# One moving operand of 512 columns for the high and low part of h in the first products of FFN and MLP

## What is computed

```python
def swiglu(h, w_gu, w_down):
    gate, up = jnp.split(h @ w_gu, 2, axis=-1)      # w_gu: 1024 x 5632
    return (jax.nn.silu(gate) * up) @ w_down        # w_down: 2816 x 1024
...
x = x + 0.5 * swiglu(rms_norm(x, norm_ffn1[i]), w_ffn1_gu[i], w_ffn1_down[i])
...
# MLP of the second network: relu(h @ w_up) ** 2 @ w_down, w_up: 1024 x 4096
```

## Time and profile before

| | |
|---|---|
| median of 3 runs | 1770.35 us (1768.21 to 1771.86) |
| profiled execution, its own time | 1772.11 us |
| its span, first to last instruction | 1770.4 us |
| mean granted TensorE clock | 0.981 |
| instructions | 31231, of them 13254 matmuls |
| raw weights | 264 units, 4.9 us median from issue to landing |

### The profile page before, as it was taken

One profiled execution on the slowest core, in us unless ns is written; L12 is line 12 of the kernel. 1 busy time (PEld: TensorE's weight loads), 2 busy tenths in 40 slices (PEclk: granted clock), 3 DMA queues, 4 the chain that ended last, 5 costly groups with the idle time before them and its releaser, 6 DMA issues.

```text
span 1770.4 us, 31231 instructions
## 1 busy us (share of the span) xinstructions
PE 1700.2 (96%) x13254; PEld 1639.6 (93%) x13254; DVE 1077.2 (61%) x1057; ACT 803.8 (45%) x942; POOL 161.1 (9%) x123
## 2 busy tenths in 40 slices
PE   7999998999999999999999999888999999989997
PEld 7999985899999999989999998768999989989997
DVE  7565676375648755486554777564655566466553
ACT  5343557353435534365343544444444455444342
POOL 1000122100002000011000243220000001100000
PEclk9999999999999999999999999789999999999999
DMA  7545451155443544445545345003454435225550
GB/s 297 193 166 189 167 190 48 72 215 195 181 174 143 217 187 185 171 178 197 214 152 204 143 177 190 1 24 120 143 191 176 179 128 187 91 101 201 177 187 24
DMA packets 39637, 282.36 MB, mean 159 GB/s; under 512 B 4416, under 2 KB 4544, under 8 KB 5760
## 3 DMA queue, kind: packets, MB, share of 16 engines
q1 hardware_dynamic: 39168, 279.59, 42.6%
q0 software_dynamic: 384, 1.51, 0.2%
HBM read 280.04 MB, written 1.05 MB: 159 GB/s over the span
## 4 chain that ended last, share of the span: by engine, by line
PE 88%; DVE 6%; ACT 3%; DMA 1%; POOL 1%; issue 1%; SPq 0%; DVEq 0%; ACTq 0%; POOLq 0%
PE ps L312 27%; PE ps L313 27%; PE ps L314 27%; DVE w_lo L1342 1%; PE ps L396 1%; ACT arena L1154 1%; ACT w_hi L970 1%; PE ps L610 1%; PE ps L654 1%; DMA raw<-weights 1%; DVE hT_lo L1354 0%; POOL arena L2011 0%; DVE arena L1643 0%; DMA arena<-nsa_tables 0%; DVE X L1481 0%
## 5 line engine op out<-in xcount | busy, mean ns | idle before, releaser
L312 PE MATMUL ps<-hT_hi,w_hi 128*128 128x256 f32 x2504 | 715.7, 286 | 22.6 <-DVE hT_lo L1354 18.0
L313 PE MATMUL ps<-hT_lo,w_hi 128*128 128x256 f32 x2504 | 710.8, 284 | 0.0
L314 PE MATMUL ps<-hT_hi,w_lo 128*128 128x256 f32 x2504 | 710.5, 284 | 0.0
L1342 DVE TENSOR_TENSOR w_lo<-raw,w_hi 128x2048 fp32r<-128x2048 f32 x264 | 601.0, 2300 | 138.6 <-ACT w_hi L970 138.5
L970 ACT ACTIVATE w_hi<-raw 128x2048 fp32r<-128x2048 f32 x264 | 495.0, 1902 | 52.0 <-DMA raw<-weights 46.0
L312 PEld LDWEIGHTS ps<-hT_hi,w_hi 128*128 128x128 f32 x2504 | 482.4, 193 | 26.1 <-DVE w_lo L1342 11.2
L313 PEld LDWEIGHTS ps<-hT_lo,w_hi 128*128 128x128 f32 x2504 | 482.9, 193 | 0.8 <-issue 0.7
L314 PEld LDWEIGHTS ps<-hT_hi,w_lo 128*128 128x128 f32 x2504 | 482.9, 193 | 0.0
L312 PE MATMUL ps<-hid_hi,w_hi 128*128 128x256 f32 x1272 | 360.5, 283 | 3.6 <-DVE hid_lo L1442 2.6
L313 PE MATMUL ps<-hid_lo,w_hi 128*128 128x256 f32 x1272 | 361.0, 284 | 0.0
L314 PE MATMUL ps<-hid_hi,w_lo 128*128 128x256 f32 x1272 | 356.1, 280 | 0.0
(11 more groups left out here) (257 smaller groups left out, 1451.5 us busy)
## 6 DMA issues: line engine op xcount, KB each, us to landing
raw<-weights SPq DMA_DIRECT2D x264, 1024.0 KB, 4.9
X<-x SPq DMA_DIRECT2D x2, 512.0 KB, 6.8
out<-X SPq DMA_DIRECT2D x4, 256.0 KB, 2.1
arena<-p POOLq DMA_DIRECT2D x2, 256.0 KB, 5.9
arena<-counts POOLq DMA_DIRECT2D x1, 512.0 KB, 5.5
arena<-nsa_tables POOLq DMA_DIRECT2D x1, 448.0 KB, 7.1
const<-constants SPq DMA_DIRECT2D x1, 427.0 KB, 9.6
cols<-parameters SPq DMA_DIRECT2D x1, 213.5 KB, 2.6
```

What stands on the lines that cost most here:

```text
L312: nc.tensor.matmul(dst, a_hi, b_hi, start=start, stop=False, skip_group_check=True)
L313: nc.tensor.matmul(dst, a_hi, b_lo, start=False, stop=False, skip_group_check=True)
L314: return nc.tensor.matmul(dst, a_lo, b_hi, start=False, stop=stop, skip_group_check=True)
L1342: nc.vector.tensor_tensor(unit_cols(w_lo, u, 0, UNIT), raw[:, r * UNIT:(r + 1) * UNIT], f(unit_cols(w_hi, u, 0, UNIT)), ALU.subtract).then ...
```

## The change

The high and low part of h now lie in one tensor, and `both(k)` gives chunk k of both as one moving operand of two runs of 256 columns. In `wide` one matmul multiplies it by w_hi into a whole bank: w_hi by h_hi goes to the first half, w_hi by h_lo to the second. A second matmul adds w_lo by h_hi to the first half. The halves are added afterwards: ScalarE copies the second halves of two banks to SBUF (`take_low`), VectorE adds the first ones (`add_low`) and signals `added` or `second_added`. A tile takes a whole bank now, so a block of the FFN takes four banks and the MLP's blocks alternate between banks 0, 1 and 2, 3.

The FFN's units are laid out anew: u holds the gate's columns, u+1 the up columns, each with all eight chunks. The first FFN block (`first_wide`) goes through both units chunk by chunk and waits for the second unit at the start; the second block lies in banks 4 to 7, which `down` enters afterwards. The last FFN block keeps the old form (`up` with two tiles into banks 0 and 1). The square in the MLP takes in the relu. The orders on ScalarE and VectorE at a stage's opening and in the loops are rewritten.

```diff
+        def both(k):
+            return hT[:].rearrange("p (a x) -> p a x", a=2)[:, :, k * TOKENS:(k + 1) * TOKENS]
+        LOW = [at(0, 512), at(512, 512)]
...
+            def wide(b, u, a, k):
+                nc.tensor.matmul(by_tile(bank(b)), unit_cols(w_hi, u, a, P), both(k), start=k == 0, stop=False, skip_group_check=True)
+                return nc.tensor.matmul(bank(b, 0, TOKENS), unit_cols(w_lo, u, a, P), chunk(hT_hi, k), start=False, stop=k == KC - 1, skip_group_check=True)
+            def up_wide(u, b0, t=None, mid={}):
+                unit_ready(u, t)
+                for k in range(KC):
+                    if k in mid:
+                        mid[k]()
+                    for m in range(2):
+                        mm = wide(b0 + m, u, (2 * k + m) * P, k)
+                mm.then_inc(unit_used.sem, 1)
+            def first_wide(us, banks, mid={}):
+                for k in range(KC):
+                    if k in mid:
+                        mid[k]()
+                    if k == 0:
+                        unit_ready(us[1])
+                    pe.wait_ge(*hT_ready.due(me))
+                    for j, u in enumerate(us):
+                        for m in range(2):
+                            mm = wide(banks[j] + m, u, (2 * k + m) * P, k)
+                        if k == KC - 1:
+                            mm.then_inc(unit_used.sem, 1)
...
-            def down(u, h, first, last, t=None, squares=False):
+            def down(u, h, first, last, t=None, squares=False, free=None):
...
+                    if free and b == 2:
+                        pe.wait_ge(*free)
...
             # TensorE, ffn
-                one(0, u0, mid={6: lambda: sums(s)})
-                one(1, u0 + 2, mid={2: lambda: spread(7)})
+                def one(u, t):
+                    pe.wait_ge(*added.due(me, turn=t))
+                    up_wide(u, 0, t)
+                    pe.wait_ge(*second_added.due(me, turn=t))
+                    up_wide(u + 1, 2, t)
+                    down(u + 2, 0, False, False, t)
+                first_wide([u0, u0 + 1], (0, 2), {6: lambda: sums(s)})
+                up_wide(u0 + 2, 4, None, {4: lambda: spread(7)})
+                pe.wait_ge(rstd_read.sem, norm_of[s] + 1 - plain)
+                up_wide(u0 + 3, 6)
+                pe.wait_ge(*added.due(me, 2))
+                down(u0 + 4, 0, True, False, free=second_added.due(me, 2))
...
             # TensorE, mlp
-                sums(s)
-                up([u0 + 2], 2, 2, None, False, mid={5: lambda: spread(7)})
-                down(u0 + 3, 0, True, False)
+                first_wide([u0, u0 + 1], (0, 4))
+                sums(s, 2)
+                up_wide(u0 + 2, 6, None, {2: lambda: spread(2)})
+                down(u0 + 3, 0, True, False, free=added.due(me, 3))
...
             # ScalarE, ffn: the opening, then a turn of the loop
+                take_low(0, 0, u0 + 2)
+                take_low(2, 1, u0 + 2)
+                split_to(u0 + 8)
+                take_low(4, 0, u0 + 3)
+                silu(0)
+                round_hidden(0)
+                split_to(u0 + 9)
+                silu(1)
+                take_low(6, 1, u0 + 4)
+                split_to(u0 + 10)
+                round_hidden(0, u0 + 5)
...
+                    take_low(0, 0, u + 1, t)
+                    split_to(u + 6, t)
+                    silu(j, t)
+                    split_to(u + 7, t)
+                    take_low(2, 1, u + 2, t)
+                    split_to(u + 8, t)
+                    round_hidden(0, u + 3, t)
...
             # VectorE, ffn: the opening, then a turn of the loop
+                split_to(u0 + 4)
                 mean_square(7)
+                add_low(gates[0], 0, 0, added)
+                add_low(second, 2, 1, second_added)
                 split_to(u0 + 5)
                 take_rstd(7)
+                scale(gates[0])
+                scale(second)
+                hidden(0)
+                add_low(gates[1], 4, 0, added)
+                scale(gates[1])
+                low_hidden(0)
+                split_to(u0 + 6)
+                add_low(second, 6, 1, second_added)
+                scale(second)
+                hidden(1)
+                split_to(u0 + 8)
+                low_hidden(0)
+                split_to(u0 + 10)
...
+                    add_low(gates[j % 2], 0, 0, added, t)
+                    scale(gates[j % 2], t)
+                    split_to(u + 6, t)
+                    add_low(second, 2, 1, second_added, t)
+                    scale(second, t)
+                    hidden(j, t)
+                    split_to(u + 7, t)
+                    low_hidden(0, t)
+                    split_to(u + 8, t)
...
             # VectorE, mlp: the opening
+                split_to(u0 + 5)
+                mean_square(2)
+                add_low(SUMS[0], 0, 0, added)
+                add_low(SUMS[1], 4, 1, added)
+                take_rstd(2)
+                squares(0)
+                low_hidden(0)
+                squares(1)
+                add_low(SUMS[0], 6, 0, added)
...
+            def take_low(b0, n, used, t=None):
+                act.wait_ge(unit_used.sem, used + (t.i * t.units if t else 0))
+                nc.scalar.activation(by_tile(LOW[n]), pair(b0, 1), ACT.Copy).then_inc(low_taken.sem, 1)
...
+            def add_low(dst, b0, n, sig, t=None):
+                dve.wait_ge(*low_taken.due(me, turn=t))
+                nc.vector.tensor_tensor(by_tile(dst), pair(b0, 0), by_tile(LOW[n]), ALU.add).then_inc(sig.sem, 1)
```

More of the change, by code:

```diff
@@ L443, in ffn @@
             def ffn(s, u0):
[L445 to L449, removed]
-                one(0, u0, mid={6: lambda: sums(s)})
-                one(1, u0 + 2, mid={2: lambda: spread(7)})
+                plain = sum(kind in ("stick", "pool") for kind, _ in stages[:s])
+                def one(u, t):
[4 more added lines that the diff above has]
+                    down(u + 2, 0, False, False, t)
@@ L461, in ffn @@
                 down(u + 3, HC, False, True)
             def mlp(s, u0):
[L466 to L474, removed]
@@ L487, in mlp @@
+                up_wide(u, 2)
+                added.due(me, 2)
                 down(u + 1, HC, False, False)
@@ L1011, in ffn, with silu @@
             def ffn(s, u0):
-                def one(j, u, t=None):
-                    more = t.i * t.units if t else 0
+                def silu(j, t=None):
+                    gate = sil[:, j % 2 * 512:j % 2 * 512 + 512]
                     act.wait_ge(*scaled.due(me, turn=t))
[L1017 to L1026, removed]
@@ L1033, in ffn, with one @@
                     for b in range(2):
-                        one(2 + b, u + 3 * b, t)
-                scaled.due(me, 2 * 3)
-                hid_ready.due(me, 2 * 3)
+                        one(b, u + 3 * b, t)
+                all_of(me, (scaled, hid_ready), 2 * 3)
                 split[me] += 3 * 6
                 u += 24
-                one(FFN_BLOCKS - 1, u)
+                split_to(u + 6)
+                silu(FFN_BLOCKS - 1)
+                split_to(u + 7)
+                round_hidden(HC)
             def mlp(s, u0):
[L1043 to L1051, removed]
-                    nc.scalar.activation(chunk(hid_hi, j % 2 * HC, HC), at(ACT_AT, 512), ACT.Copy).then_inc(hid_hi_done.sem, 1)
-                    split_to(ahead, t)
-                one(0, u0 + 1, u0 + 6)
-                one(1, u0 + 2, u0 + 7)
-                one(2, u0 + 3, u0 + 8, free=u0 + 4)
+                def one(b, u, t=None):
+                    take_low((b + 1) % 2 * 2, (b + 1) % 2, u + 1, t)
+                    split_to(u + 5, t)
+                    round_hidden((b + 1) % 2 * HC, u + 2, t)
+                    split_to(u + 6, t)
+                take_low(0, 0, u0 + 1)
+                take_low(4, 1, u0 + 2)
+                split_to(u0 + 7)
+                round_hidden(0)
+                take_low(6, 0, u0 + 3)
+                round_hidden(HC)
+                split_to(u0 + 8)
+                round_hidden(0, u0 + 4)
                 u = u0 + 4
```

132 lines of the change are left out of this document (78 added, 54 removed).

## The result

The changed kernel takes 1824.81 us (median of 4 runs, 1823.1 to 1828.33) against 1769.28 us of the kernel before on the same chip (1767.07 to 1771.86): 1.0316 times as long, interval 1.0294 to 1.0338. The forecast was 1820, slower. The profiled execution took 1828.33 us, 56.2 more than the profiled one before; the forecast of that difference was 49.4.

The account below looks back on a forecast made before the run. TensorE, working without holes, was taken as the bound. On the profiled 1772.11 us, -22.9 + 5.0 + 61.5 + 8.4 - 2.6 = +49.4 gave 1821.5, or 1819.7 as median; own range 1804 to 1836, wider range 1785 to 1840.

Parts of the forecast that it names:

- Pace of a group: FFN and MLP matmul groups: 347.2 ns instead of 360, 12.8 ns less in 1792 groups, 22.9 us won.
- Rival (c): Matmul groups: the two-run operand streams at the pace of two matmuls, nothing won, 1843 us; chance 0.11.
- rival (d): Matmul groups: a long matmul costs no more than a short one, 240 ns a group, 1628 us; chance 0.01.
- Start: Program start: TensorE waits for the second unit before its first matmul, at a low clock; cost 5.0 us.
- Openings: Four FFN stage openings: TensorE stalls at the first `down` behind late raw-weight landings; 61.5 us lost, 53 to 70.
- the two gaps: Each FFN opening's first `down`: TensorE stands 3.6 us for the hidden block, then 8.2 us for the last add.
- Clock: After each FFN opening's second gap: low clock costs 2.1 us, 8.4 us in all, between 0 and 16.
- MLP opening: Two MLP stage openings: TensorE's 1.3 us wait for the first hidden block goes; 2.6 us won, 0 to 2.6.
- Rival (a): FFN openings: transfers released one low part earlier, so openings are hidden and the kernel faster, 1750 to 1759 us; chance 0.12.

Follow-up runs that it names:

- two long, two short: Changed kernel with two long matmuls, then two short ones, per chunk and pair of tiles, instead of alternating them: 1825.55 us, 1.0309 times before.
- reordered: Changed kernel with ScalarE's and VectorE's orders at the four FFN stage openings rearranged, same instructions: 1766.39 us, 0.9987 times before.
- both: Changed kernel with the FFN openings reordered and two long matmuls, then two short ones: 1758.59 us, 0.9948 times before.
- one low part moved ahead: Changed kernel with VectorE making the low part of u0+4 ahead of the two adds in FFN openings, plus a ScalarE wait: 1805.82 us, 1.0200.

## Why the prediction was right, point by point

**Pace of a group.** The two paces that it read from the earlier trace rows were right: the long matmul of two runs takes 227.5 ns among its like. The term was mis-sized: -22.9 us. In the trace a group saves 6.9 ns and not 12.8, 12.4 us over 1792 groups; the `down` steps, at 117.5 ns, give some 7 more. That second part was in no forecast, so that the term comes near is partly luck. By turns it is 0.35 us for each of 40 FFN blocks and 0.17 for each of 32 MLP blocks (turns of 11.28 and 11.41 us in turn, after 11.52), 19.5 us. The pace was taken from stretches of one kind each; that alternation costs was not a bound in the text. With two long, two short a group saves 11.9 ns, and there the `down` stays at 120. The Trainium skill ("TensorE: Matmul & The Clock Gate", Back-to-back issue gap) gives about 2.5 ns above the columns for an isolated warm matmul, which makes an estimate of 4.5 us. The rows have more than that in either order: 6.9 and 11.9 ns a group. Rival (c) would have 360 ns and rival (d) 240 ns a group: both fall.

**Start.** TensorE starts at 16.45 (16.3 forecast), after the earlier trace rows 11.21. The first low stretch lasts 6 us, not 4.4, and the first two units end at 31.0, not 29.8. Before, they would end at 25.0 with the cheaper groups, so the cost is 6.0 where 5.0 were forecast. The timeline of the changed kernel has the end of the stretch, by the length of the wide matmuls:
```profile
21.74 0.63 PE L364 MATMUL ps<-hT,w_hi 128*128 128x512 f32 x1
...
22.38 0.42 PE L364 MATMUL ps<-hT,w_hi 128*128 128x512 f32 x1
```
Up to 21.74 a wide matmul takes 0.63 us, from 22.38 on some 0.40. The length of this stretch is not the change's own: in traces of kernels with the same start it is 2.8 us (two long, two short), 5.0 (reordered) and 6.0 (both).

**Openings.** The walk through both queues holds. From S = 31.2, where ScalarE takes up the low halves, the first hidden block is ready at S+14.4 (15.2 forecast) and the last add at S+25.2 (26.3), since the two landings take 4.75 and 4.91 us and not 5.04, and the other steps are a little shorter too. The gaps and those for the scale factors (L1450) or the sums of squares sum to 9.1, 12.5, 13.3 and 12.7 us in the four stages, 47.6. Between the two gaps the half of the `down` took 4.6, 5.5, 4.6 and 3.1 us for 2.9, because the clock was low: another 6.2, which the prediction counted in the second gap. 53.8 for 61.5; by stage 10.8, 15.1, 15.0 and 12.9 us for 12.1, 17.0, 18.8 and 13.6. The stall moves nothing else: in the loops TensorE waits for no one. That the openings and not something else made the loss is shown by the reordered kernel, which differs in nothing else and takes 58.4 us less; which of the two queues' edits does how much is shown for the low part of u0+4 alone.

**Clock.** The shares missing in the four windows behind the long gaps are 1.7, 2.4, 1.9 and 2.5 us, 8.5 for 8.4. Not foreseen: a low stretch behind the wait for the scale factors in the fifth stage and behind the sums of squares in the seventh, 2.1 and 1.7 us by the same view (0.73 of 7.8 us from 622.3; 0.79 of 8.0 us from 850.0), 3.8 together. The one of the fifth stage costs nothing of its own: TensorE then stands 2.56 us for the hidden block, and would stand longer by as much without it, so these 2.1 us belong to the opening's price. The one of the seventh delays the first two units, for which ScalarE then waits 2.33 us.

**MLP opening.** Each MLP stage is 4.3 us shorter; 16 blocks at 0.17 and the 1.3 of the earlier trace rows make 4.1. TensorE's wait for `hid_lo` there is gone.

**Not foreseen:** the attention stage ahead of the first MLP is 4.7 us longer (236.9 for 232.2), with a granted clock of 0.88 for 0.90 and the same instructions. The kernel with only the MLP changed does the work of the one before up to the end of that stage and takes 229.1 us there in its trace. So this stage's length moves by microseconds between traces without an edit, and the 4.7 us are not shown to be the change's.

**The sum.** Forecast -22.9 + 5.0 + 61.5 + 8.4 - 2.6 = 49.4. Measured -19.5 + 6.0 + 53.8 + 12.3 - 2.6 + 4.7 = 54.7 of 56.2; 1.5 are in no term. The total is near because openings that were priced too high are offset by a start, clock stretches and an attention stage that were priced too low or not at all, and by groups that win less than forecast, so it is no proof of the single terms; the rows above are. Rival (a) was not what the kernel did, but what it does once reordered: it was priced at 1750 to 1759, and 1766.39 and 1758.59 were measured with its gaps gone.

## What to carry to other kernels

When an edit reorders an in-order queue, walk each queue at the opening of a stage with the landing times in it: a step that waits for a transfer should stand behind all work that the bottleneck's next step needs, and the step that releases the transfer ahead of it. Here that was worth some 57 us, three times the 19.5 us that the cheaper groups won. Judge a gain per instruction by the whole turn of the loop, not by the edited step: 5 ns a group were won and handed to the `down`. An early start of a stage gained nothing here, where the next waits in it were for other engines.

## What the runs showed of the hardware

- A long and a short matmul in turn take 353.1 ns, a long one among long ones 227.5 and a short one among short ones 120.0, together 347.5. In three blocks of the changed kernel the two in turn take 346.6 ns. In pairs of each kind it is 348.1.
- A moving operand of two runs of 256 columns costs no more than one of 512.
- The same `down` instructions run at 117.5 ns in some loops and at 120.0 in others, and with long and short in turn each FFN loop keeps its pace to its end. It is not a matter of the kernel: all four FFN stages of the changed kernel have 117.5 and all four of the reordered one 120.0, but with one low part moved ahead the first and third stage have 117.5, the fifth and seventh 120.0. Two turns of that kernel, `down` and the first long matmul behind it:
```profile
101.70 0.28 PE L327 MATMUL ps<-hid_hi,w_hi 128*128 128x256 f32 x1
...
107.33 0.39 PE L364 MATMUL ps<-hT,w_hi 128*128 128x512 f32 x1
...
661.59 0.28 PE L327 MATMUL ps<-hid_hi,w_hi 128*128 128x256 f32 x1
...
667.35 0.40 PE L364 MATMUL ps<-hT,w_hi 128*128 128x512 f32 x1
```
- The first `down` takes 5.63 us and the second 5.76. In the MLP of the changed kernel turns of 11.28 and 11.41 us alternate. With two long, two short the loops have 120.0 from their second turn at the latest. Which state of the engine decides it was not found; it moves a comparison of two kernels by up to 4 us (0.12 us in each of 32 FFN turns) without any edit to the `down`.
- After most gaps of 1.8 to 7.6 us in TensorE's work the granted clock was low for some microseconds, but not after all: it was 1.00 over the 6.0 us behind the gap of 2.94 us in the third stage and over the 3.2 us behind the one of 3.33 us in the seventh.
- At the start of the program the low stretch lasted 6 us where the kernel before had 4.4; with an unchanged start it was 2.8 to 6.0 us in other kernels of this case.
